# A MoE layer's prompt output summed in PSUM banks 4 to 7, and a gather that scales in its selection matrix

## What is computed

```python
x = x + mix
x = x + moe(rmsnorm(x, norm_ffn_g), w_router, b_router, w_up, b_up, w_down, b_down)
# moe: y = sum over the chosen experts of gate * (act(xs @ w_up[e] + b_up[e]) @ w_down[e] + b_down[e])
def rmsnorm(x, g):
    return x * lax.rsqrt(jnp.mean(x * x, axis=-1, keepdims=True) + EPS) * g
y_prompt = rmsnorm(xp, norm_final_g)
y_sample = rmsnorm(xs, norm_final_g)
```

## Time and profile before

| | |
|---|---|
| median of 3 runs | 1273.46 us (1272.34 to 1274.46) |
| profiled execution: its time / its span | 1271.02 us / 1269.2 us |
| PE busy, share of the span | 1152.5 us, 91% |
| PEld | 586.8 us, 46% |
| DVE | 676.7 us, 53% |
| POOL | 653.9 us, 52% |
| ACT | 244.0 us, 19% |
| HBM read | 447 MB, 354 GB/s over the span |

### The profile page before, as it was taken

How to read it: one execution, slowest core, us unless ns; L and a number is a source line. 1 busy time by engine, 2 the same in 40 slices (tenths; PEclk the granted TensorE clock), 3 DMA queues, 4 the chain that set the end, 5 groups by cost and what they waited for, 6 DMA issues and landing times.

```text
span 1269.2 us, 30932 instructions
## 1 busy us (share of the span) xinstructions
PE 1152.5 (91%) x11113; PEld 586.8 (46%) x11114; DVE 676.7 (53%) x1256; ACT 244.0 (19%) x487; POOL 653.9 (52%) x709
## 2 busy tenths in 40 slices
PE   8999999999999989799797998997997879979895
PEld 7777777775444334243332443432433324434332
DVE  2999984121755635545342557553554445535534
ACT  2012124001222212122121221221221212212122
POOL 1012300000566858749671687586585756857863
PEclk9999999999999999999898999998998989989998
DMA  9974443336999999999999799999999999999996
GB/s 263 349 242 129 163 129 117 114 142 278 380 385 397 396 422 422 421 422 422 422 422 422 282 400 424 422 422 422 422 422 422 422 422 422 422 422 422 422 422 277
DMA packets 94539, 448.91 MB, mean 354 GB/s; under 512 B 8502, under 2 KB 42870, under 8 KB 45315
## 3 DMA queue, kind: packets, MB, share of 16 engines
q1 hardware_dynamic: 94078, 447.21, 87.8%
q10 hardware_dynamic: 437, 1.39, 0.3%
HBM read 447.00 MB, written 2.42 MB: 354 GB/s over the span
## 4 chain that ended last, share of the span: by engine, by line
PE 60%; DMA 18%; DVE 17%; issue 3%; DVEq 1%; ACT 1%; POOL 0%; SPq 0%; POOLq 0%; ACTq 0%
PE banks L1372 21%; DMA ring<-in_w_down 17%; PE banks L1382 13%; DVE staging L803 8%; PE banks L1167 8%; PE banks L1089 5%; PE banks L1147 4%; PE banks L1126 3%; PE banks L1283 2%; PE banks L1133 2%; PE banks L1156 1%; DMA staging<-in_w_up 1%; DVE hT L1036 1%; DVE hT L1029 1%; DVE staging L812 1%
## 5 line engine op out<-in xcount | busy, mean ns | idle before, releaser
L524 POOL COPY ring<-staging 128x1024 f32<-128x1024 f32 x620 | 623.8, 1053 | 472.0 <-PE banks L1372 372.4
L1372 PE MATMUL banks<-ring,hT 128*32 128x512 f32 x3328 | 414.8, 604 | 12.7 <-DVE hT L779 7.5
L330 DVE TENSOR_TENSOR xt<-xt,banks 128x1024 f32<-128x1024 f32 x106 | 128.7, 1215 | 371.7 <-PE banks L1147 371.7
L1382 PE MATMUL banks<-ring,hT 128*32 128x256 f32 x3328 | 229.1, 395 | 73.3 <-DMA ring<-in_w_down 64.4
L1382 PEld LDWEIGHTS banks<-ring,hT 128*32 128x32 f32 x3328 | 109.6, 114 | 249.7 <-issue 136.3
L1167 PE MATMUL banks<-hT,ring 128*128 128x288 f32 x768 | 188.4, 406 | 0.3 <-ACT hT L561 0.3
L1372 PEld LDWEIGHTS banks<-ring,hT 128*32 128x32 f32 x3328 | 104.8, 111 | 149.9 <-issue 106.8
L1167 PEld LDWEIGHTS banks<-hT,ring 128*128 128x128 f32 x768 | 145.1, 190 | 39.7 <-issue 0.4
L683 ACT COPY WT<-banks 128x256 f32<-128x256 f32 x52 | 19.4, 372 | 533.8 <-PE banks L1382 533.8
L803 DVE SCALAR_TENSOR_TENSOR staging<-staging 128x256 f32<-128x256 f32 x240 | 107.4, 522 | 0.0
L762 DVE TENSOR_SCALAR WT<-slot_ids,prod 128x32 f32 x156 | 81.5, 581 | 0.0
(11 more groups left out here) (245 smaller groups left out, 737.0 us busy)
## 6 DMA issues: line engine op xcount, KB each, us to landing
staging<-in_w_up SPq DMA_DIRECT2D x248, 1024.0 KB, 18.5
ring<-in_w_down SPq DMA_DIRECT2D x66, 1024.0 KB, 11.1
staging<-in_w_down SPq DMA_DIRECT2D x62, 1024.0 KB, 18.4
ring<-in_w_in SPq DMA_DIRECT2D x24, 1024.0 KB, 10.3
ring<-in_w_up SPq DMA_DIRECT2D x8, 1024.0 KB, 4.8
ring<-in_w_branch_b SPq DMA_DIRECT2D x4, 1024.0 KB, 5.4
ring<-in_w_branch_a SPq DMA_DIRECT2D x4, 1024.0 KB, 4.9
ring<-in_w_out SPq DMA_DIRECT2D x4, 1024.0 KB, 5.0
```

Source lines behind the costliest of these rows:

```text
L330: nc.vector.tensor_tensor(dst, dst, rows, ALU.add).then_inc(y_added, 1)
L524: ins = nc.gpsimd.tensor_copy(ring[:, k, half], staged[k][:, half])
L1372: ins = mm(UP[g * BLK:(g + 1) * BLK, :], xT[:, k, :], ring[:, k, g * 512:(g + 1) * 512], start=k == 0, stop=k == UP_SLOTS - 1)
L1382: ins = mm(DN[q * BLK:(q + 1) * BLK, 0:256], actT[:, f % 4, f // 4, :], ring[:, UP_SLOTS + j, h * D + q * 256:h * D + (q + 1) * 256], star ...
```

## The change

The outputs of the two prompt tiles are no longer added to xt by VectorE after each combine. PE puts xt itself into banks 4 to 7 once, by an identity matmul (`start_rows`), and all combines of the prompt tiles accumulate there (start=False), to the last one. The squares and the final scaling read the banks. Only the sample's output is still added by VectorE, under a semaphore of its own. `keep_rows` becomes `invert_root`: no scaled rows are kept, the gather reads xt, and `select` multiplies the 0/1 matrix by the inverse root (ss columns 4 and 5) for the prompt tiles.

```diff
-            def keep_rows(tt):
+            def invert_root(tt):
...
-                dve.wait_ge(inverted2, tt + 1)
-                if tt < 2:
-                    V.tensor_scalar(stage[:, tt, :], xt[:, tt, :], col2, None, ALU.mult).then_inc(rows_kept, 1)
...
-                for tt in range(NT):
-                    ins = V.tensor_scalar(sel[:, tt, :], slot_ids[:, bass.ds(rank0, BLK)],
-                                          rankm[:, tt, bass.ds(expert, 1)], None, ALU.is_equal)
-                ins.then_inc(sel_ready, 1)
+                for tt in range(2):
+                    V.tensor_scalar(sel[:, tt, :], slot_ids[:, bass.ds(rank0, BLK)],
+                                    rankm[:, tt, bass.ds(expert, 1)], ss[:, 4 + tt:5 + tt], ALU.is_equal, ALU.mult)
+                V.tensor_scalar(sel[:, 2, :], slot_ids[:, bass.ds(rank0, BLK)],
+                                rankm[:, 2, bass.ds(expert, 1)], None, ALU.is_equal).then_inc(sel_ready, 1)
...
-                add_before(i, 1)
-                dve.wait_ge(combined, i * NT + (NT + 1))
-                add_output(dve, row_out[0], 0)
...
+            def start_rows():
 
                 for q in range(QN):
-                    ins = mm(rows[:, q, :],
+                    mm(bank[4 + q].rearrange("p (t n) -> p t n", t=2), ident[:], x_cols[:, q], start=True, stop=False)
+
+            def combine(tt, last=False):
+
+                for q in range(QN):
+                    ins = mm(y_rows[tt][:, q, :],
                              combT[q * BLK:(q + 1) * BLK, tt * P:(tt + 1) * P],
-                             out_sb[q * BLK:(q + 1) * BLK, :], start=True, stop=True)
-                ins.then_inc(combined, 1)
...
+            start_rows()
             pe.wait_ge(bdown_in, 16 * QN)
             pe.wait_ge(combT_ready, 1)
-            combine(0, row_out[0])
+            combine(0)
...
-                        pe.wait_ge(y_added, i * NT + 2)
+                        pe.wait_ge(sample_added, i + 1)
...
+            act.wait_ge(rows_combined, 1)
             for tt in range(2):
-                act.wait_ge(y_added, bodies * NT + (NT + tt + 1))
-                nc.scalar.activation(stage[:, tt, :], xt[:, tt, :], ACT.Square, accum_out=ss[:, tt:tt + 1]
+                nc.scalar.activation(squares[tt], y_rows[tt], ACT.Square, accum_out=ss[:, tt:tt + 1]
                                      ).then_inc(squared3, 1)
-                act.wait_ge(squared3, tt + 1)
-                root(ss[:, 4 + tt:5 + tt], ss[:, tt:tt + 1], 1.0 / D, rooted2)
+            act.wait_ge(squared3, 2)
+            root(ss[:, 4:6], ss[:, 0:2], 1.0 / D, rooted2)
```

More of the change, by code:

```diff
@@ L185, in carve @@
             return regs[region][0:rows, lo:lo + n]
+        squares = [regs["hT"][:, tt * D:(tt + 1) * D].rearrange("p (q n) -> p q n", q=QN) for tt in range(2)]
         xT = carve("hT", KC * BLK).rearrange("p (k t) -> p k t", k=KC)
@@ L208, in hybrid_layer @@
         fing, fingq = ring[:, 0, 0:D], ring[:, 0, D:D + 256]
-        stageq = stage[:, 2, 0:256]
+        xq_rows = stage[:, 2, 0:256]
+        x_cols = xt[:].rearrange("p t (q n) -> p q t n", q=QN)
         banks = ctx.enter_context(nc.psum_tensor("banks", [P, 8, 512], F32))
@@ L657, in _ @@
             act.wait_ge(x2_ready, 5)
-            nc.scalar.activation(stageq, xq[:], ACT.Square, accum_out=ss[:, 2:3]).then_inc(quarters_squared, 1)
+            nc.scalar.activation(xq_rows, xq[:], ACT.Square, accum_out=ss[:, 2:3]).then_inc(quarters_squared, 1)
             act.wait_ge(quarters_summed, 1)
@@ L661, in _ @@
             act.wait_ge(inverted2, 3)
-            nc.scalar.mul(stageq, xq[:], ss[:, 6:7]).then_inc(rows_kept, 1)
+            nc.scalar.mul(xq_rows, xq[:], ss[:, 6:7]).then_inc(rows_kept, 1)
             act.wait_ge(shifted, 1)
@@ L952, in _ @@
             route(1)
-            keep_rows(2)
+            invert_root(2)
             route(2)
@@ L1132, in gather_sample @@
                     row = slice(q * NS, (q + 1) * NS)
-                    ins = mm(XB[row, 0:256], sel[row, 2, :], stageq[row, :], start=False, stop=True)
+                    ins = mm(XB[row, 0:256], sel[row, 2, :], xq_rows[row, :], start=False, stop=True)
                 ins.then_inc(gathered, 1)
@@ L1395, in combine_before @@
             def combine_before(i):
-                pe.wait_ge(y_added, i * NT + 1)
-                combine(1, row_out[1])
-                combine_sample(DN[:, 256:512])
+                combine(1)
+                combine_sample()
             def turn_weights(i):
@@ L1461, in _ @@
             pe.wait_ge(out_ready, bodies + 1)
-            pe.wait_ge(y_added, bodies * NT + NT)
-            for tt in range(2):
-                combine(tt, tail_out[tt])
-            pe.wait_ge(y_added, bodies * NT + (NT + 1))
-            tr(Y0[:, 256:384], ident[:])
-            combine_sample(Y0[:, 256:512])
+            combine(0)
+            combine(1, last=True).then_inc(rows_combined, 1)
+            combine_sample()
             pe.wait_ge(quarters_squared, 2)
-            pe.wait_ge(y_added, bodies * NT + (NT + 2))
             sum_quarters(UP[:, 0:1])
```

83 lines of the change are left out of this document (40 added, 43 removed).

## The result

The changed kernel takes 1277.11 us (median of 20 runs), the kernel before 1274.4 us beside it: ratio 1.0022, 95% interval 1.0014 to 1.003, so 2.8 us slower, with 1.8 to 3.8 us as the interval. The forecast was +2.3 us, and its mechanism is there. It named 1275.8 us; of the 1.3 us to the measured time, 0.9 us are the base (1273.46 us, the median of three runs, against 1274.4 us) and 0.4 us the change. But the profile also holds a loss of 1.7 us in the tail that the forecast did not see.

What follows compares the result with a forecast made beforehand. The prediction took saturated weight DMA to bound two stretches and PE two others. Start +2.3, loop 0 and tail 0 sum to +2.3 us on 1273.46, giving 1275.8 us; 8-in-10 range 1272.8 to 1278.4 us.

Steps and rivals of the forecast that it cites:

- What bounds the kernel: Whole span: saturated weight DMA sets the pace in two stretches, PE in two others; a PE delay at 338-432 us carries through.
- The additions at nothing: In the loop: removing 106 VectorE additions, 128.7 us of its time, gains 0, hidden by its wait for the up-projection.
- Accumulating: Combines adding to banks 4 to 7 instead of overwriting them: cost 0.
- the rival of the lost overlap: In PE-bound stretches: accumulating products run one after another, 23.6 us more, 1297 us; chance 0.03.
- The selection: Before and in the loop: second scalar in two comparisons, scaled rows no longer kept; 0, bounds -0.1 and +0.3 us.
- start_rows: Ahead of the first combine: four products cost 3.43 us on PE, 2.3 us after give-backs; bounds 2.0 and 3.4.
- Both give-backs: First loop block: gather 3.0 us late instead of 3.43; first down product 2.3 us late, VectorE running behind GpSimd's copies.
- The tail at 0: After the last combines: first scaling 0.54 us later, sample's scaling where it is now; 0, bounds -0.3 and +0.6 us.
- a sign of being right: In the tail: the sample's scaling starts 7.1 to 7.7 us after the last combine's start.
- The surcharge for reading PSUM: The tail's two scalings: 0.13 us more by the skill page's figures, left out of the sum.
- the forecast's sum by rows: In the tail: profile rows show no PSUM surcharge (1215 against 1222 ns), so scalings stay at 1.28 us each.

Runs made afterwards that it cites:

- after_unseeded: The changed kernel without the four identity products, the first combine overwriting the banks instead: ratio 1.0008 to the kernel before.
- before_products: The kernel before with the four identity products put ahead of the first combine, their result overwritten, nothing else changed: ratio 1.0020 to the kernel before.
- after_tail_busy: The changed kernel with five dummy products of 256 columns on PE while it waits for the last block's activation: ratio 1.0012 to the kernel before.
- before_small_adds: The kernel before with VectorE's additions of the prompt rows' output cut to 8 of each quarter's 256 columns: ratio 0.9995 to the kernel before.
- after_again: The changed kernel once more, unchanged, for comparison and a second profile: ratio 1.0014 to the kernel before.
- after_hidden: The changed kernel with its four identity products moved from before the first combine to earlier places where TensorE waits: ratio 1.0021 to the kernel before.
- after_more_start: The changed kernel with eight more identity products of 128x512 in front of the four, 12 instead of 4: ratio 1.0076 to the kernel before.
- after_product_each: The changed kernel with one more identity product of 128x512 in each of the loop's 51 turns, behind combine(0): ratio 1.0076 to the kernel before.

## Why the prediction was right, and where it was not

- **What bounds the kernel.** Right, and shown by two doses: 6.9 us of TensorE's work ahead of the loop cost 6.9 to 7.9 us, 44 us of it spread over the loop cost 5.3 to 8.2.
- **The additions at nothing.** Right. VectorE's waits took them up, and cutting them alone gave 0.9995. But one of the reasons given, that TensorE's waits for the additions "had been satisfied before it came to them", did not hold at the end: the trace of before has a wait of 0.54 us for one. The additions held two places in queues: TensorE's 0.54 us wait ahead of the last block's combine of tile 1, and VectorE's sequencer at the loop's entry.
- **Accumulating.** Right at 0: eight instructions of a combine take 0.71 us before and after, and the rival of the lost overlap (1297 us) falls.
- **The selection.** Right at 0. Two scalars made the groups dearer, 612 ns against 581 in the mean, but in after_unseeded the gather still waited 0.69 us for it, as against 0.67 before.
- **start_rows.** The four products took 3.63 us to the combine's start (3.43 forecast from the pitch of the mixer's), and the first up-projection of this profile lay 0.39 us later than in the profile before. With that taken off, the gather was at 341.65 us (forecast 341.75), the first down product at 348.76 us (348.8 to 348.99), the load at 353.47 us (353.6). The start measures 19.50 - 17.33 = 2.17 us against 2.3 forecast. Both give-backs came, but two misses offset each other in the first: the products were 0.20 us longer than forecast, and the 0.3 us expected from the combine to the gather were absent (0.65 us from start to start, all of it the combine's). That the gather came within 0.1 us is in part luck. The second came as derived, 0.73 us with line 1029 at 0.41 us. One condition of it was not stated: that VectorE reaches its activation in time was assumed "with the same steps before it". That held only because the additions were gone (before_products: 3.16 us).
- **The tail at 0** is the step that failed. Its parts behind the last combines were followed, and came out a little shorter than forecast: 7.32 instead of 7.65 us to the sample's store, in part since the second square followed the first after 1.00 us and not 1.18. The sample's scaling stood 6.81 us behind the start of the last combines, outside the 7.1 to 7.7 us named as a sign of being right. The step began too late, at the last combines. It left out that the wait of TensorE for VectorE that goes (0.54 us) lies ahead of a wait that stays, the last block's for the activation. Nothing is gained by arriving earlier there: the down products start 4.91 us behind the activation's transposes now, 4.78 before. The idle time becomes longer, and behind it the clock was granted at half: +1.69 us. The trace of before had such a fall already, inside the loop, behind a wait for a load; 16 down instructions took 1.71 us there and 1.07 in other blocks (the row of the timeline, and the window behind it):

```profile
449.98 1.71 PE L1382 MATMUL banks<-ring,hT 128*32 128x256 f32 x16 [3.35 <-DMA ring<-in_w_down]
450.00:452.00 2.00, 2.00 (x20) 0.94 (x24) 0.00 (x0) 0.00 (x0) 1.65 (x2) 0.57 1.02 422
```

- **The surcharge for reading PSUM**, 0.13 us as an estimate by the Trainium skill's page "VectorE: DVE Perf Modes", section "The TRN2 errata — SBUF-src ops pay a fixed extra latency per instruction", can't be seen: each scaling took 1.28 us, as the forecast's sum by rows has it. The squares on ScalarE took 1.00 and 1.01 us from PSUM, 1.06 and 1.04 from SBUF before.

The sum by the traces is 2.17 at the start, 0.13 and 1.69 at the last down products and -0.33 behind them: +3.7 us. Measured were +2.8 (1.8 to 3.8) and +1.8 (0.6 to 2.9), so the sum lies inside the first interval and above the second. The forecast of +2.3 lies between the two, and that is in part luck: the clock's loss, which it lacked, is offset by something that no experiment isolated. Over eleven comparisons with the kernel before such sums lie on average 0.6 us above what the ratios say (after_unseeded 1.6 against 1.0, after_tail_busy 2.0 against 1.5, before_small_adds 0.9 against -0.6, at the very end of its interval). The sums also leave out the stretch from the first down product to the last block's, where single profiles differ by up to 2.7 us. This stays open.

## What to carry to other kernels

Before an edit is costed at nothing because its engine waits anyway, list what stands behind it in the queues of both engines: the removed addition had no price as work, but it held VectorE's register instructions back at one place and split TensorE's idle time in two at another. A wait that is removed ahead of a wait that stays gives back nothing, and gathers idle time in one piece, for which TensorE can pay in its clock. When an added piece of work commutes with the rest, as an accumulated x does, put it where the engine idles on the critical path and not where it is first possible.

## What the runs showed of the hardware

- TensorE's granted clock fell to 0.50 behind 2.10 to 2.41 us of idle time in six profiles of five kernels (the change, after_again, after_unseeded, after_hidden, after_more_start, before_small_adds), 64 instructions taking 5.35 instead of 3.66 us. It did not fall behind 1.67 us (three profiles), nor behind 2.27 us in after_product_each, and not where the gap was filled. What decides between these cases is open.
- Register instructions of VectorE that stand behind a waiting instruction took from 343.5 to 346.3 us to catch up at the loop's entry in before_products, and the activation behind them started 0.70 us later than in the change.
- Beside GpSimd's copies the same VectorE instruction of 256 columns with two SBUF inputs took 1.25 us, behind them 0.41 us, and which of the two holds is decided by when TensorE releases it.
